# Four of six pieces of each expert's down matrix as fp16 halves in the gate-up ring, two as fp32 matmuls

## The chip, the cores and the metric

One core of one Trainium2 chip runs one inference step of a two-layer decoder. The metric is the time of one execution on the device in microseconds (us): 1238.76 us, the median of three runs (1237.88 to 1239.49). Lower is better.

## The reference

264 tokens (256 of a prompt and 8 samples) of width 1024 go through two layers. Each has a mixer, and then a feed-forward part: dense in the first layer, a mixture of experts in the second. Everything is fp32. What matters here is the mixture:

```python
def swiglu(x, w_gu, w_dn):
    g, u = jnp.split(x @ w_gu, 2, axis=-1)
    return (jax.nn.silu(g) * u) @ w_dn

def moe_swiglu(x, router, w_gu, w_dn):
    """Top-2-of-8 SwiGLU experts, softmax over the selected logits, per token."""
    ...
    for e in range(N_EXPERTS):
        out = out + comb[..., e:e + 1] * swiglu(x, w_gu[e], w_dn[e])
    return out
```

For each of the 8 experts `w_gu[e]` is 1024 x 3072 (12 MB) and `w_dn[e]` 1536 x 1024 (6 MB).

## The kernel before, in words

**Weights.** All weights come from memory as fp32 in pieces of 1 MB (128 partitions x 2048 numbers). Most are not multiplied as fp32. A piece is split: ScalarE writes the fp16 part of 256 times the weight to `wh` (`hi_gu`, L940), and VectorE the fp16 rest to `wl` (`lo_gu`, L1266). TensorE then does three fp16 matmuls for one product: high weight by high input, high weight by low input, low weight by high input (L844 to L846). `wh` and `wl` are a ring of four slots (`SLOTS`); a split waits until TensorE has used the piece four places before it (L939).

**One expert.** The matrix `w_gu[e]` is 12 pieces (`GU_U`), in three blocks of four; a piece has 96 matmuls with 128 weight columns against the expert's up to 96 tokens (`CAP`). From the sums in the four banks of `acc` ScalarE makes a tanh (`gates`, L1196) and VectorE the hidden values (`gate` L1762, `hidden_e` L1775, into `hid_e`, fp32, three parts q of four chunks). The matrix `w_dn[e]` is 6 pieces (`DN_U`). They are not split: `down` (L859) multiplies them as fp32, 96 columns of `hid_e` as weights and 512 columns of the piece moving, four matmuls a piece, straight from the slot where the transfer put it. There are six slots for gate-up pieces as loaded and five for down pieces.

**Order of work.** It is written out by hand and the same loop, for e from -1 to 7 and for turns g from 0 to 5, stands in each engine's program; an engine does its instructions in that order, and semaphores tie them together. In a turn TensorE does two gate-up pieces of expert e+1, and down piece g of expert e. In turns 0 and 1 it also scatters expert e-1's output back to the tokens (`scatter`, L805 and L806, two chunks before the down piece and two after), and VectorE adds these to the residual (`add_scattered`, L1751). In turn 2 TensorE gathers the tokens of expert e+2 (`gather`, L790 and L794, two banks before the down piece and two after), and ScalarE copies them out (`gathered`, L1180). Gathers, transposed selections (`by_token`, L724) and scatters take turns in two banks of `aux`: a fill waits until the one two before it has been read (`fill_bank`). In turn g ScalarE and VectorE split the gate-up pieces that are four ahead of the two that TensorE does. After turn 5 ScalarE scales the expert's output (L1229), in two halves, and VectorE makes its rest (`expert_out`, L1783), which the scatters of the next expert's turns and its first down piece wait for. The lines of ScalarE's program at this place, before the change:

```python
for g in range(DN_U):
    if e + 2 < NE and g == 3:
        gathered(e + 2, 2)
        gathered(e + 2, 3)
    for j in ((e + 1) * GU_U + 2 * g + SLOTS, (e + 1) * GU_U + 2 * g + SLOTS + 1):
        if j < GU_ALL:
            hi_gu(j)
    ...
    if e + 2 < NE and g == 2:
        gathered(e + 2, 0)
        gathered(e + 2, 1)
```

**Transfers.** SyncE's queue issues them in a fixed order: two gate-up pieces (L368), which wait for VectorE's split six pieces before, and a down piece (L382), which waits for TensorE's matmuls of the down piece five before. Fillers (`keep_warm`, L581) are fp16 matmuls of 512 columns whose result isn't used.

## Time and profile before

| | before |
|---|---|
| median of three runs | 1238.76 us (1237.88 to 1239.49) |
| the profiled execution | 1241.73 us |
| its span in the trace | 1240.1 us |
| TensorE busy | 1211.8 us (98%) |
| VectorE busy | 871.0 us (70%) |
| ScalarE busy | 629.4 us (51%) |
| clock granted to TensorE, of full | 0.979 |

The span is the part of the execution that the trace covers; all times in the rows count from its start. A row's duration of a matmul includes the time in the pipeline, so that matmuls that follow each other overlap, and the distance of two starts tells what one costs. The experts' loop runs from about 745 to 1190 us.

### The profile page before, as it was taken

Reading aid. Unit: us, or ns where it says so; the run is one execution under the profiler, and the core shown is the slowest. Engines: PE = TensorE matmul, PEld = TensorE weight load, DVE = VectorE, ACT = ScalarE, POOL = GpSimd, SP = SyncE. Lnnn points to the kernel's source line nnn. Section 1 sums busy time; section 2 is a strip of 40 time slices with the busy share of each in tenths; the row PEclk is TensorE's granted clock in tenths of the full one; section 3 lists DMA queues with packets and bytes.
Section 4 is the critical chain, followed back from the end, with each engine's and each line's share of the span. In section 5 each row is a group of like instructions: output and inputs, shape, how many; then the busy total and the mean of one; then the engine's idle time right before and its main releaser. Section 6 shows DMA issues by size and latency. Waiting matters only on the chain.

```text
span 1240.1 us, 27339 instructions
## 1 busy us (share of the span) xinstructions
PE 1211.8 (98%) x11977; PEld 957.4 (77%) x11977; DVE 871.0 (70%) x962; ACT 629.4 (51%) x613; POOL 24.9 (2%) x59
## 2 busy tenths in 40 slices
PE   7999999999999999999999989999999999999988
PEld 4888888878888887888888847876777777777556
DVE  5986886876666578977886785857557575747366
ACT  4555644455554455555744455645445454545233
POOL 4000000000000001000000000000000000000000
PEclk7999999999999999999999997999999999999999
DMA  9665665646555654465666647899898897988601
GB/s 263 204 218 189 203 202 181 200 136 204 194 185 197 204 170 153 137 204 181 202 199 203 238 157 282 328 370 384 314 374 330 318 400 307 376 325 328 235 1 36
DMA packets 171067, 289.31 MB, mean 233 GB/s; under 512 B 5195, under 2 KB 132187, under 8 KB 170954
## 3 DMA queue, kind: packets, MB, share of 16 engines
q1 hardware_dynamic: 169242, 283.71, 64.9%
q0 software_dynamic: 1728, 4.16, 1.2%
q8 instruction: 78, 1.28, 0.4%
q14 instruction: 19, 0.16, 0.0%
HBM read 286.53 MB, written 1.52 MB: 232 GB/s over the span
## 4 chain that ended last, share of the span: by engine, by line
PE 89%; DVE 7%; ACT 2%; issue 1%; DMA 0%; ACTq 0%; SPq 0%; DVEq 0%
PE acc L554 15%; PE acc L556 15%; PE acc L555 15%; PE aux L859 14%; PE acc L844 6%; PE acc L846 5%; PE acc L845 5%; PE aux L790 3%; PE acc L539 2%; PE acc L546 2%; PE acc L540 2%; DVE wl L1260 1%; DVE xb L1340 1%; PE aux L643 1%; DVE rstd L1321 1%; PE aux L594 1%
## 5 line engine op out<-in xcount | busy, mean ns | idle before, releaser
L554 PE MATMUL acc<-xn,wh 128*128 128x264 f16 x1424 | 393.0, 276 | 0.6 <-DVE wl L1260 0.6
L555 PE MATMUL acc<-xn,wh 128*128 128x264 f16 x1424 | 393.0, 276 | 0.0
L556 PE MATMUL acc<-xn,wl 128*128 128x264 f16 x1424 | 393.0, 276 | 0.0
L1260 DVE SCALAR_TENSOR_TENSOR wl<-raw,wh 128x2048 f16<-128x2048 f32 x124 | 283.5, 2289 | 104.9 <-ACT wh L931 104.4
L931 ACT ACTIVATE wh<-raw 128x2048 f16<-128x2048 f32 x124 | 235.6, 1903 | 0.1
L844 PE MATMUL acc<-ga,wh 128*128 128x96 f16 x1536 | 212.2, 212 | 0.2 <-issue 0.2
L845 PE MATMUL acc<-ga,wh 128*128 128x96 f16 x1536 | 212.0, 212 | 0.0
L846 PE MATMUL acc<-ga,wl 128*128 128x96 f16 x1536 | 212.0, 212 | 0.0
L1266 DVE SCALAR_TENSOR_TENSOR wl<-raw,wh 128x2048 f16<-128x2048 f32 x64 | 144.3, 2287 | 62.4 <-ACT wh L940 62.4
L940 ACT ACTIVATE wh<-raw 128x2048 f16<-128x2048 f32 x64 | 122.0, 1910 | 101.5 <-PE acc L846 97.8
L845 PEld LDWEIGHTS acc<-ga,wh 128*128 128x128 f16 x1536 | 155.6, 101 | 7.8 <-issue 7.6
L844 PEld LDWEIGHTS acc<-ga,wh 128*128 128x128 f16 x1536 | 155.5, 101 | 6.7 <-issue 6.4
L554 PEld LDWEIGHTS acc<-xn,wh 128*128 128x128 f16 x1424 | 139.3, 98 | 21.7 <-ACT wh L931 0.8
L555 PEld LDWEIGHTS acc<-xn,wh 128*128 128x128 f16 x1424 | 139.3, 98 | 21.1
L846 PEld LDWEIGHTS acc<-ga,wl 128*128 128x128 f16 x1536 | 155.6, 101 | 0.0
L556 PEld LDWEIGHTS acc<-xn,wl 128*128 128x128 f16 x1424 | 139.3, 98 | 20.9
L975 ACT ACTIVATE ot<-acc 128x528 f32<-128x528 f32 x47 | 28.6, 609 | 124.3 <-PE acc L556 97.3
L1266 DVE SCALAR_TENSOR_TENSOR wl<-sa,wh 128x2048 f16<-128x2048 f32 x16 | 36.7, 2291 | 44.4 <-ACT wh L940 44.4
L790 PE MATMUL aux<-ga,w 128*128 128x96 f16 (+1 forms) x384 | 46.1, 219 | 3.3 <-issue 3.2
L940 ACT ACTIVATE wh<-sa 128x2048 f16<-128x2048 f32 x16 | 30.6, 1910 | 36.8 <-PE acc L846 36.8
L790 PEld LDWEIGHTS aux<-ga,w 128*128 128x128 f16 (+1 forms) x384 | 27.2, 96 | 25.0 <-issue 6.9
L554 PE MATMUL acc<-w,wh 128*128 128x264 f16 x144 | 39.7, 276 | 0.0
(278 smaller groups left out, 1692.8 us busy)
## 6 DMA issues: line engine op xcount, KB each, us to landing
raw<-in_moe_w_gu SPq DMA_DIRECT2D x64, 1024.0 KB, 9.6
raw<-in_w_in SPq DMA_DIRECT2D x56, 1024.0 KB, 5.1
raw<-in_ffn_w_gu SPq DMA_DIRECT2D x24, 1024.0 KB, 5.2
sa<-in_moe_w_gu SPq DMA_DIRECT2D x16, 1024.0 KB, 8.5
xb<-in_moe_w_gu SPq DMA_DIRECT2D x16, 1024.0 KB, 10.4
raw<-in_ffn_w_dn SPq DMA_DIRECT2D x12, 1024.0 KB, 5.2
ya<-in_moe_w_dn SPq DMA_DIRECT2D x10, 1024.0 KB, 7.6
sg<-in_moe_w_dn SPq DMA_DIRECT2D x10, 1024.0 KB, 6.9
```

The costliest lines, as they stand in the source:

```text
L554: nc.tensor.matmul(bank, hi, x[:, 0, x0 + k, :], start=(k == 0), stop=False)
L555: nc.tensor.matmul(bank, hi, x[:, 1, x0 + k, :], start=False, stop=False)
L556: last = nc.tensor.matmul(bank, lo, x[:, 0, x0 + k, :], start=False, stop=(k == k_chunks - 1))
L790: last = nc.tensor.matmul(bank[:, at:at + CAP], nt[0:n, s, t, c * P:(c + 1) * P], sel[e % 2][0:n, t, :], start=(t == 0), stop=(t == 2))
L844: nc.tensor.matmul(bank, hi, x[:, 0, k, :], start=first, stop=False)
L845: nc.tensor.matmul(bank, hi, x[:, 1, k, :], start=False, stop=False)
L846: last = nc.tensor.matmul(bank, lo, x[:, 0, k, :], start=False, stop=end)
L859: last = nc.tensor.matmul(aux[0:CAP, 2 + half, :], hid_e[:, 2 * g + k, :], w[:, k, half * 512:(half + 1) * 512], start=(2 * g + k == 0), s ...
L931: nc.scalar.activation(wh[:, s, 0:size], raw_slot[s][:, 0:size], ACT.Copy, scale=WS).then_inc(hi_done, 1)
L940: nc.scalar.activation(wh[:, j % SLOTS, :], g_slot[j % G_SLOTS], ACT.Copy, scale=WS).then_inc(g_hi, 1)
L1260: op(V.scalar_tensor_tensor(out=wl[:, s, 0:size], in0=raw_slot[s][:, 0:size], scalar=WS, in1=wh[:, s, 0:size], op0=ALU.mult, op1=ALU.subtr ...
L1266: op(V.scalar_tensor_tensor(out=wl[:, j % SLOTS, :], in0=g_slot[j % G_SLOTS], scalar=WS, in1=wh[:, j % SLOTS, :], op0=ALU.mult, op1=ALU.su ...
```

## The change

The first four down pieces of each expert (`DN_HALVES`, g = 0 to 3) are split like gate-up pieces and take their places in the same ring of four slots, in the order in which TensorE uses the pieces: two gate-up pieces, then a down piece. ScalarE's and VectorE's splits of a turn are those four places ahead in this ring (`ring_ahead`), three in turns 0 to 3 and two in turns 4 and 5. The parts q = 0 and 1 of `hid_e` are split too (`hidden_hi` on ScalarE, `hidden_lo` on VectorE, into `hid_s`, which lies in `ot`). A split down piece is 12 fp16 matmuls (`down_halves`) instead of four fp32 ones; pieces g = 4 and 5 stay as they were. The slot of a split down piece is loaded again when VectorE has split it. The scale that takes back the 256 moves from `hid_e` to `csl`. What only renames `hid_e_ready` to `hid_made` is left out below.

```diff
+DN_HALVES = 4
+HC = 2 * DN_HALVES
+
+
+def in_halves(i):
+    return i % DN_U < DN_HALVES
+
+
+def half_ring():
+
+    order = [("g", j) for j in range(GU_U)]
+    for e in range(NE):
+        for g in range(DN_U):
+            if e + 1 < NE:
+                order += [("g", (e + 1) * GU_U + 2 * g + k) for k in range(2)]
+            if g < DN_HALVES:
+                order.append(("d", e * DN_U + g))
+    return order
+
+
+RING = half_ring()
+RING_AT = {key: n for n, key in enumerate(RING)}
+
+
+def ring_turn(e, g):
+
+    out = [("g", (e + 1) * GU_U + 2 * g + k) for k in range(2)] if e + 1 < NE else []
+    return out + ([("d", e * DN_U + g)] if e >= 0 and g < DN_HALVES else [])
+
+
+def ring_ahead(e, g):
+
+    turn = ring_turn(e, g)
+    if not turn:
+        return []
+    n = RING_AT[turn[0]] + SLOTS
+    return RING[n:n + len(turn)]
 
...
         mask_t, cum = var[0:NE, :], rtmp[0:NE, :]
+        hid_s = ot[:].rearrange("p a b t -> p (a b t)").bitcast(F16)[:, 0:2 * HC * CAP].rearrange("p (s c t) -> p s c t", s=2, c=HC)
         cmp_a, cmp_b = (x[:, 0:3 * NE * NE].rearrange("p (t m o) -> p t m o", t=3, m=NE) for x in (std, rstd))
...
         d_loaded = [sem(f"d_loaded{i}") for i in range(D_SLOTS)]
+        d_hi, d_lo, hid_hi, hid_lo = sem("d_hi"), sem("d_lo"), sem("hid_hi"), sem("hid_lo")
         g_hi, g_lo, gu_mm, dn_mm, y_half = sem("g_hi"), sem("g_lo"), sem("gu_mm"), sem("dn_mm"), sem("y_half")
 
+        def halves_to(i):
+
+            return i // DN_U * DN_HALVES + min(i % DN_U, DN_HALVES)
+
         block = ctx.enter_context(nc.Block())
...
                     sp.wait_ge(fill_full[0], 1)
+                elif in_halves(i - D_SLOTS):
+                    sp.wait_ge(d_lo, halves_to(i - D_SLOTS + 1))
                 else:
                 pe.wait_ge(g_lo, j + 1)
-                th = wh[:, j % SLOTS, :].rearrange("p (c m) -> p c m", c=2)
-                tl = wl[:, j % SLOTS, :].rearrange("p (c m) -> p c m", c=2)
+                slot = RING_AT["g", j] % SLOTS
+                th = wh[:, slot, :].rearrange("p (c m) -> p c m", c=2)
+                tl = wl[:, slot, :].rearrange("p (c m) -> p c m", c=2)
                 x = xg[e % 2]
...
 
+            def down_halves(i):
+
+                e, g = i // DN_U, i % DN_U
+                pe.wait_ge(hid_hi, HC // 4 * e + g // 2 + 1)
+                pe.wait_ge(hid_lo, HC // 4 * e + g // 2 + 1)
+                pe.wait_ge(d_hi, halves_to(i) + 1)
+                pe.wait_ge(d_lo, halves_to(i) + 1)
+                slot = RING_AT["d", i] % SLOTS
+                th = wh[:, slot, :].rearrange("p (c m) -> p c m", c=2)
+                tl = wl[:, slot, :].rearrange("p (c m) -> p c m", c=2)
+                for k in range(2):
+                    c = 2 * g + k
+                    for half in range(2):
+                        bank, s = aux[0:CAP, 2 + half, :], slice(half * 512, (half + 1) * 512)
+                        nc.tensor.matmul(bank, hid_s[:, 0, c, :], th[:, k, s], start=(c == 0), stop=False)
+                        nc.tensor.matmul(bank, hid_s[:, 0, c, :], tl[:, k, s], start=False, stop=False)
+                        last = nc.tensor.matmul(bank, hid_s[:, 1, c, :], th[:, k, s], start=False, stop=False)
+                last.then_inc(dn_mm, 1)
+
             def down(i):
...
                 e, g = i // DN_U, i % DN_U
-                pe.wait_ge(d_loaded[i % D_SLOTS], 16 * (i // D_SLOTS + 1))
-                pe.wait_ge(hid_e_ready, BLOCKS * e + g // 2 + 1)
                 if g == 0 and e:
                     pe.wait_ge(ys_ready, 2 * e)
+                if in_halves(i):
+                    down_halves(i)
+                    return
+                pe.wait_ge(d_loaded[i % D_SLOTS], 16 * (i // D_SLOTS + 1))
+                pe.wait_ge(hid_made, BLOCKS * e + g // 2 + 1)
                 w = d_slot[i % D_SLOTS].rearrange("p (c m) -> p c m", c=2)
...
             pe.wait_ge(fill_done[k % 2], k // 2 + 1)
-            pe.wait_ge(hid_e_ready, NE * BLOCKS)
             for c in range(C):
...
 
+            def ring_free(n):
+
+                kind, i = RING[n - SLOTS]
+                act.wait_ge(gu_mm if kind == "g" else dn_mm, i + 1)
+
             def hi(n, size=UNIT, it=None, step=0):
...
                 if n >= N_PLE[1]:
-                    act.wait_ge(gu_mm, GU_ALL - LEAD + (n - N_PLE[1]))
+                    ring_free(len(RING) + n - N_PLE[1])
                 elif n >= SLOTS:
...
                 act.wait_ge(g_loaded[j % G_SLOTS], 16 * (j // G_SLOTS + 1))
-                if j < SLOTS:
-                    act.wait_ge(unit_mm, N_MOE - LEAD + j)
+                n = RING_AT["g", j]
+                if n < SLOTS:
+                    act.wait_ge(unit_mm, N_MOE - LEAD + n)
                 else:
-                    act.wait_ge(gu_mm, j - LEAD)
-                nc.scalar.activation(wh[:, j % SLOTS, :], g_slot[j % G_SLOTS], ACT.Copy, scale=WS).then_inc(g_hi, 1)
+                    ring_free(n)
+                nc.scalar.activation(wh[:, n % SLOTS, :], g_slot[j % G_SLOTS], ACT.Copy, scale=WS).then_inc(g_hi, 1)
+
+            def hi_dn(i):
+
+                act.wait_ge(d_loaded[i % D_SLOTS], 16 * (i // D_SLOTS + 1))
+                n = RING_AT["d", i]
+                ring_free(n)
+                nc.scalar.activation(wh[:, n % SLOTS, :], d_slot[i % D_SLOTS], ACT.Copy, scale=WS).then_inc(d_hi, 1)
+
+            def hidden_hi(e, q):
+
+                act.wait_ge(hid_made, BLOCKS * e + q + 1)
+                nc.scalar.activation(hid_s[:, 0, 4 * q:4 * q + 4, :], hid_e[:, 4 * q:4 * q + 4, :], ACT.Copy,
+                                     scale=1.0 / WS).then_inc(hid_hi, 1)
 
                         gathered(e + 2, 3)
-                    for j in ((e + 1) * GU_U + 2 * g + SLOTS, (e + 1) * GU_U + 2 * g + SLOTS + 1):
-                        if j < GU_ALL:
-                            hi_gu(j)
+                    for kind, i in ring_ahead(e, g):
+                        if kind == "g":
+                            hi_gu(i)
+                        else:
+                            hi_dn(i)
                     if e + 1 < NE and g == 1:
...
                         by_token(e + 2)
+                    if e + 1 < NE and g in (4, 5):
+                        hidden_hi(e + 1, g - 4)
                     if e == NE - 1 and g in (2, 3, 4):
...
                 vec_e.wait_ge(g_hi, j + 1)
-                op(V.scalar_tensor_tensor(out=wl[:, j % SLOTS, :], in0=g_slot[j % G_SLOTS], scalar=WS,
-                                          in1=wh[:, j % SLOTS, :], op0=ALU.mult, op1=ALU.subtract), g_lo)
+                slot = RING_AT["g", j] % SLOTS
+                op(V.scalar_tensor_tensor(out=wl[:, slot, :], in0=g_slot[j % G_SLOTS], scalar=WS, in1=wh[:, slot, :],
+                                          op0=ALU.mult, op1=ALU.subtract), g_lo)
+
+            def lo_dn(i):
+
+                vec_e.wait_ge(d_hi, halves_to(i) + 1)
+                slot = RING_AT["d", i] % SLOTS
+                op(V.scalar_tensor_tensor(out=wl[:, slot, :], in0=d_slot[i % D_SLOTS], scalar=WS, in1=wh[:, slot, :],
+                                          op0=ALU.mult, op1=ALU.subtract), d_lo)
+
+            def hidden_lo(e, q):
+
+                vec_e.wait_ge(hid_hi, HC // 4 * e + q + 1)
+                op(V.scalar_tensor_tensor(out=hid_s[:, 1, 4 * q:4 * q + 4, :], in0=hid_e[:, 4 * q:4 * q + 4, :],
+                                          scalar=1.0 / WS, in1=hid_s[:, 0, 4 * q:4 * q + 4, :], op0=ALU.mult,
+                                          op1=ALU.subtract), hid_lo)
 
...
                 vec_e.wait_ge(fill_done[k % 2], k // 2 + 1)
-                op(V.tensor_tensor(csl[0:CAP, e:e + 1], csr[0:CAP, e, 0:1], csr[0:CAP, e, 1:2], ALU.add), csl_ready)
+                op(V.tensor_scalar(csl[0:CAP, e:e + 1], csr[0:CAP, e, 0:1], csr[0:CAP, e, 1:2], UNSCALE, ALU.add, ALU.mult),
+                   csl_ready)
 
...
                 op(V.scalar_tensor_tensor(out=hid_e[:, 4 * q:4 * q + 4, :].rearrange("p c t -> p (c t)"), in0=w,
-                                          scalar=0.5 * UNSCALE * UNSCALE, in1=acc[:, block % 2 * 2 + half, 0:GW],
-                                          op0=ALU.mult, op1=ALU.mult), hid_e_ready)
+                                          scalar=0.5 * UNSCALE, in1=acc[:, block % 2 * 2 + half, 0:GW],
+                                          op0=ALU.mult, op1=ALU.mult), hid_made)
 
...
                                           in1=ye[0:CAP, 0, s], op0=ALU.mult, op1=ALU.subtract), ys_ready)
+
+            def split(kind, i):
+                if kind == "g":
+                    lo_gu(i)
+                else:
+                    lo_dn(i)
 
...
                 for g in range(DN_U):
-                    first = (e + 1) * GU_U + 2 * g + SLOTS
+                    ahead = ring_ahead(e, g)
                     if g == 0 and 2 <= e + 2 < NE:
...
                         slot_weights(e + 2)
-                    if first < GU_ALL:
-                        lo_gu(first)
+                    if ahead:
+                        split(*ahead[0])
                     if e >= 1 and g < 2:
...
                         add_scattered(e - 1, 4 * g + 1)
-                    if first + 1 < GU_ALL:
-                        lo_gu(first + 1)
+                    for key in ahead[1:]:
+                        split(*key)
                     if e + 1 < NE:
...
                             hidden_e(block, 0)
+                        if g in (4, 5):
+                            hidden_lo(e + 1, g - 4)
                     if e >= 1 and g < 2:
```

## Rows read from the trace of the kernel before

**Rows 1.** The page: busy time of TensorE, its share and instructions.

```profile
PE 1211.8 (98%) x11977; PEld 957.4 (77%) x11977; DVE 871.0 (70%) x962; ACT 629.4 (51%) x613; POOL 24.9 (2%) x59
```

**Rows 2.** Busy time by stretch, from one expert's first gate-up piece to the next.

```profile
core 0: us, PE busy (x) PEld busy (x) DVE busy (x) ACT busy (x) POOL busy (x), PEclk, DMA share, GB/s
895.98:950.71 54.73, 54.73 (x696) 39.11 (x694) 34.62 (x33) 27.49 (x23) 0.00 (x0) 0.97 0.89 349
```

**Rows 3.** Waits in 895.98 to 950.71: engine, line, releaser; us, times, longest.

```profile
ACT wh L940 <- PE acc L846: 19.9, 7, 4.5
DVE wl L1266 <- ACT wh L940: 14.8, 6, 4.8
```

**Rows 4.** Timeline of TensorE: start, duration, line, operation, shapes, count.

```profile
884.95 3.64 PE L859 MATMUL aux<-ya,w 128*96 128x512 f32 x8
...
888.43 0.21 PE L844 MATMUL acc<-ga,wh 128*128 128x96 f16 x1
...
892.51 3.64 PE L859 MATMUL aux<-sg,w 128*96 128x512 f32 x8
...
916.90 2.74 PE L790 MATMUL aux<-ga,w 128*128 128x96 f16 x24
...
923.08 2.74 PE L790 MATMUL aux<-ga,w 128*128 128x96 f16 x24
...
926.06 0.22 PE L844 MATMUL acc<-ga,wh 128*128 128x96 f16 x1
...
931.75 0.41 PE L724 MATMUL aux<-identh,ga 128*96 128x128 f16 x3
```

**Rows 5.** Timeline of TensorE, one run of fillers.

```profile
735.03 1.91 PE L581 MATMUL acc<-identh 128*128 128x512 f16 x8
```

**Rows 6.** Instructions of line L724: durations ns min/median/max.

```profile
L724 PEld LDWEIGHTS aux<-identh,ga x24: 114/123/195, 753.0 to 1096.1; 128*96 128x96 f16 x16, 8*96 8x96 f16 x8
```

**Rows 7.** Groups of instructions by line in 895.98 to 950.71: busy us, mean ns.

```profile
L845 PEld LDWEIGHTS acc<-ga,wh 128*128 128x128 f16 x192 | 19.4, 101 | 1.0 <-issue 1.0
```

**Rows 8.** Timeline of VectorE.

```profile
913.74 1.01 DVE L1762 SCALAR_TENSOR_TENSOR w<-w,acc 128x384 f32<-128x384 f32 x2
914.67 0.76 DVE L1751 SCALAR_TENSOR_TENSOR h<-aux,h 128x264 f32<-128x264 f32 x2
917.07 4.49 DVE L1266 SCALAR_TENSOR_TENSOR wl<-raw,wh 128x2048 f16<-128x2048 f32 x2 [1.64 <-ACT wh L940]
...
1167.67 0.77 DVE L1751 SCALAR_TENSOR_TENSOR h<-aux,h 128x264 f32<-128x264 f32 x2 [2.91 <-PE aux L806]
```

**Rows 9.** Timeline of ScalarE.

```profile
918.98 0.47 ACT L1180 ACTIVATE ga<-aux 128x384 f16<-128x384 f32 x1
...
1162.15 0.68 ACT L1229 ACTIVATE gb<-aux,csl 96x512 f16<-96x512 f32 x1 [0.97 <-PE aux L859]
1162.74 5.50 ACT L931 ACTIVATE wh<-raw 128x2048 f16<-128x2048 f32 x3
```

**Rows 10.** Timeline of TensorE near the end of the experts.

```profile
1167.36 0.27 PE L806 MATMUL aux<-gb 96*128 96x264 f16 x1
1167.47 0.28 PE L805 MATMUL aux<-gb 96*128 96x264 f16 x1
...
1168.16 0.29 PE L805 MATMUL aux<-gb 96*128 96x264 f16 x1 [0.30 <-DVE h L1751]
```

**Rows 11.** Busy time by stretch, columns as in rows 2 (PEclk: granted clock).

```profile
740.00:760.00 20.00, 16.38 (x168) 12.15 (x169) 4.88 (x16) 9.26 (x15) 0.00 (x0) 0.66 0.80 310
...
926.00:932.00 6.00, 6.00 (x100) 5.91 (x100) 0.46 (x2) 2.46 (x3) 0.00 (x0) 0.72 1.02 416
```

**Rows 12.** Waits of the queue that issues transfers, 700 to 1190.

```profile
SPq L382 <- PE aux L859: 305.4, 43, 11.1
```

**Rows 13.** Busy time of one short stretch, columns as in rows 2.

```profile
908.00:912.00 4.00, 4.00 (x28) 2.09 (x25) 3.35 (x4) 3.28 (x4) 0.00 (x0) 1.00 1.02 410
```

More of the change, by code:

```diff
@@ L89 @@
 FILL = aux_fills()
+DN_HALVES = 4
[13 more added lines that the diff above has]
+RING_AT = {key: n for n, key in enumerate(RING)}
+assert len(RING) % SLOTS == 0
+def ring_turn(e, g):
[7 more added lines that the diff above has]
+    return RING[n:n + len(turn)]
 def program(nc, a, o):
@@ L213, in program @@
         d_loaded = [sem(f"d_loaded{i}") for i in range(D_SLOTS)]
+        d_hi, d_lo, hid_hi, hid_lo = sem("d_hi"), sem("d_lo"), sem("hid_hi"), sem("hid_lo")
         g_hi, g_lo, gu_mm, dn_mm, y_half = sem("g_hi"), sem("g_lo"), sem("gu_mm"), sem("dn_mm"), sem("y_half")
-        tanh_done, gate_free, hid_e_ready = sem("tanh_done"), sem("gate_free"), sem("hid_e_ready")
+        tanh_done, gate_free, hid_made = sem("tanh_done"), sem("gate_free"), sem("hid_made")
         fill_full = [sem(f"fill_full{i}") for i in range(2)]
@@ L826, in gate_up @@
                     else:
-                        pe.wait_ge(hid_e_ready, BLOCKS * before + 2 * b - 1)
+                        pe.wait_ge(hid_made, BLOCKS * before + 2 * b - 1)
                 if u == 0:
@@ L1193, in gates @@
                 if block and block % BLOCKS == 0:
-                    act.wait_ge(hid_e_ready, block)
+                    act.wait_ge(hid_made, block)
                 at = (block % BLOCKS * 2 + half) * GW
```

## The prediction

> **What bounds the kernel now.** I read the page's busy shares first: TensorE is busy for 98% of the span [rows 1]. Then the stretches of single experts: from one expert's first gate-up piece to the next it is 54.73 us, TensorE has no idle time in it, VectorE works 34.6 and ScalarE 27.5 us, the granted clock is 0.97 and the 16 DMA engines are 0.89 busy at 349 GB/s [rows 2]. So experts are bound by TensorE. The waits say how close the others are: ScalarE waits 19.9 us for TensorE to free a slot of the ring, VectorE 14.8 us for ScalarE, per expert [rows 3]. The other engines are early, but only by what the ring lets them be, and that is what the change touches.
>
> **What the change takes from TensorE.** A down piece of four fp32 matmuls shows as eight instructions, 884.95 to 888.43, 3.48 us; a pair of gate-up pieces 888.43 to 892.51, 4.08 us, 2.04 each [rows 4]. The new piece is 12 fp16 matmuls of 512 columns. Such matmuls stand in the trace as fillers: eight in 1.91 us with a last one of 0.38 are 7 steps in 1.53, 0.218 us each [rows 5], so 2.61 us a piece and 0.87 less than now. 4 pieces x 8 experts x 0.87 = 27.8 us off TensorE.
> Its weights have 96 columns. A fp16 load of that width takes 0.12 us [rows 6]; hidden under 0.218 of matmul it costs nothing, wholly exposed 12 x 0.12 = 1.44 a piece and 46 us in all. I take nothing: the gate-up matmuls, at 4.08/96 = 0.043 each, run over loads of 0.10 [rows 4, 7]. Below nothing it can't go, as the twelve steps are the fillers' own.
> The Trainium skill (TensorE: Matmul & The Clock Gate, Back-to-back issue gap) gives about 131 ns for a sustained 512-column matmul. By it a piece would be 1.57 us. The fillers here contradict it; it stands as a rival below.
>
> **What it adds elsewhere.** 32 splits on ScalarE at 1.80 us from start to start (three in 5.50 with a last of 1.91) and on VectorE at 2.20 (two in 4.49, the last 2.29) [rows 8, 9]; 16 small ones of hid_e on each, which I price like a gate of 384 columns, 0.46 (two in 1.01) [rows 8]. VectorE then works 34.6 + 4 x 2.2 + 2 x 0.46 = 44.3 us per expert, ScalarE 27.5 + 4 x 1.8 + 0.8 = 35.5, against 54.73 - 4 x 0.87 = 51.25 of TensorE. On the average it fits. But the ring has still four slots and now three pieces a turn (g = 0 to 3) where there were two, so a piece is split 1.3 turns ahead, not 2. Both engines take work in written order, so other things queue behind a split that waits. Latencies: from the end of a matmul's slot to its dependant 0.2 us (L805 at 1167.47 follows the L806 of 1167.36; VectorE starts at 1167.67), ScalarE to VectorE 0.04, VectorE to TensorE 0.05 (the add started 1167.67 is 0.43 long, L805 at 1168.16) [rows 8, 10].
>
> **Stall A, certain by the order.** In turn g = 2 ring_ahead gives pieces g7 and g8 of expert e+1 and d3 of e, in the order g7, d3, g8. g8 takes the slot of d2, which is this turn's own down piece. ScalarE has gathered(e+2, 0) behind that split, and TensorE's gather 2, which follows d2 directly, waits for it because it writes the same bank. After d2 ends: 0.2 + 1.81 (split) + 0.48 (gathered, 0.47 long) [rows 9] + 0.05 = 2.55 us of idle TensorE. Before, both splits of that turn wait for gate-up pieces only, and gathered starts at 918.98, 4.1 us ahead of gather 2 at 923.08 [rows 4, 9]. Experts e = 0 to 5 have it: 6 x 2.55 = 15.3 us.
>
> **Stall B.** In turn g = 1 the last split, g6, takes the slot of d1. Behind it on VectorE stand two gates and add_scattered 6; gather 0 of the next turn wants the bank of that add. After d1: 0.2 + 1.91 + 0.04, split 2.20, two gates 0.92, add 0.42 [rows 8], 0.05: 5.74. TensorE gets there after four scatter matmuls (0.11 each [rows 10]) and a gate-up pair: 0.45 + 4.08 = 4.53. Stall 1.2, for e = 1 to 5: 6.0 us.
>
> **Stall C.** Scatter matmuls of turns 0 and 1 need VectorE's adds for their banks, and the adds stand behind splits. From the end of the expert before, turn 0 runs: VectorE ends a last split at 1.0 and does hidden by 1.5; ScalarE halves it by 2.1, scales two halves of the output (0.6 each, 0.68 long [rows 9]) by 3.3 and splits g3 by 5.2; VectorE splits it by 7.4 and adds by 7.8. TensorE would want that bank at 4.08 + 0.45 + 2.61 = 7.1: stall 0.7. Then VectorE: add 1 8.2, two splits 12.6, add 2 13.0; TensorE 7.8 + 0.6 + 4.08 = 12.5: 0.5. With the second adds of each pair (0.1 each) 1.3 per expert, for e = 1 to 6: 7.8 us. Bounds per expert 0, if the chain starts 1 us sooner, and 2.6, if it starts 1.3 later.
>
> **Ends.** In the first expert VectorE starts behind, as gate-up alone asks 2.20 of it per 2.04 of TensorE; with d0 (2.2) and two hidden splits (0.5 each) on top g15 is late by about 2.8. At e = 6 the scale of the expert's output (ScalarE L1229 [rows 9]) is queued behind hidden_hi(7, 1), which waits for VectorE's hidden, itself behind three splits: about 3 us more than now. Together 5.8, bounds 0 and 9.
>
> **Clock.** At 926.06 a gate-up pair takes 5.69 instead of 4.08; the clock in 926 to 932 is 0.72, part of it at the lower of the two levels, 1.2 GHz, right after gather (24 matmuls from 916.90), down and gather (from 923.08) [rows 4, 11]. There are five such places (e = 1 to 5), 1.6 us each, 8 us. The stretch from the first gather is lengthened by 2.55 of idle and has Stall B ahead of it. In 740 to 760, with TensorE busy 16.4 of 20 us, it was 0.66 [rows 11]. So I expect seven or eight drops for five: +4 us. Bounds: -8 (none, because the fp16 piece between the gathers keeps the clock) and +16 (two per expert).
>
> **Transfers.** SP waits 305 us at L382 for down pieces that TensorE has read [rows 12]; four of six slots are now free at the split, before the matmuls. An expert's 18 pieces of 1.05 MB take 18.9 / 0.40 = 47 us at the 400 GB/s of a stretch in which the DMA engines are full (410 at a share of 1.02) [rows 13], under 51. I count nothing. If they sustained only the mean of 349 GB/s [rows 2]: 54 us, and no gain could come whatever the engines do.
> UNSCALE moved into csl, one tensor_scalar for a tensor_tensor, one wait less at the end of the experts: nothing, under VectorE's idle time there.
>
> **Sum.** -27.8 + 15.3 + 6.0 + 7.8 + 5.8 = +7.1; with the clock +11. The profiled execution took 1241.73 us with a span of 1240.1; it becomes 1252.8, which stands as that one did 3.0 over the median. Forecast 1238.8 + 11.1 = 1250 us. Range of this case alone 1243 to 1262.
>
> **Rivals.**
> 1. *The other engines keep up* (ends on the other side). VectorE's 44.3 of 51 us per expert fits, B, C and the ends vanish, only A stays: -27.8 + 15.3 = -12.5, with the clock as it is 1226 us. For it: 14.8 us of waiting per expert in which VectorE has nothing to do [rows 3]. Against it: those waits are for slots, and slots are scarcer now. It decides once B, C and the ends together stay under 8.5 us, where I have 19.6. 9%.
> 2. *The clock stays up.* With A to C as above and no drop at all: 1238.8 + 7.1 - 8 = 1238: no change. For it: dense fp16 instead of fp32 between the gathers. Against: more idle. 7%.
> 3. *Weight loads are exposed.* 0.12 a matmul makes the piece 4.05: 32 x 0.57 = 18 dearer than the old one where a gain of 28 stood, while A stays and some of B and C is covered: 1238.8 + 18 + 15 + 10 = 1282 us. For it: 24 gather matmuls of 96 columns take 2.74 us, 0.11 each, where gate-up's take 0.043 [rows 4]. Against: these change between 128 and 8 rows, the new ones don't. 5%.
> 4. *The page's 131 ns.* TensorE gives back 32 x 1.91 = 61 us, but VectorE and the slots then bind: of the further 33 us about half is waited away, 1233 us. 2%, since the fillers show 0.218.
> 5. *Transfers bind*: at 349 GB/s 54 us plus the drops, 1250 to 1258; not to be told from the forecast by time, only by ScalarE waiting on DMA. 7%.
> The forecast has 70%.
>
> **Chances.** A measurement of this kernel can tell about 0.2%, 2.5 us. Slower: the forecast (nearly all), 3 and 5: 81%. Same: 2 and the lowest edge of the forecast: 8%. Faster: 1 and 4: 11%. Range 1238 to 1264: it leaves out rival 1, 3 and 4 and the tails.
>
> **What would show it.** In the expert stretches: the period from gate-up to gate-up about 56 to 57 us instead of 54.73; down pieces of 2.6 us in g = 0 to 3; TensorE idle 2.5 us after d2, released by ScalarE's ga (L1180's successor); 1.2 us before gather 0 and under a microsecond before scatters, released by VectorE's adds; VectorE over 80% busy. Wrong would be: no idle time before gather 2, a period under 53 us, down pieces of 3.5 us or more, or ScalarE's splits waiting for DMA.

## The result and the profile after

The changed kernel takes 1270.48 us, median of four executions (1266.84 to 1275.58), against 1239.12 before (four executions as well): ratio 1.0254 [1.0225, 1.0282]. In a later set of runs the same kernel took 1272.97 us (1267.25 to 1275.64), ratio 1.0264 [1.0224, 1.0303]. Forecast were 1250 us and 1238 to 1264: slower, as said, but by 31 us instead of 11, and outside the range. The profile below is of the fastest of the four executions; the second profile, of the later set, is of the slowest there (1275.64).

The page of the changed kernel, to be held against [rows 1]: span, busy time, and the chain that ended last.

```profile
span 1265.2 us, 27755 instructions
PE 1201.7 (95%) x12105; PEld 966.9 (76%) x12105; DVE 950.4 (75%) x1010; ACT 693.1 (55%) x661; POOL 24.9 (2%) x59
...
PE 73%; DVE 19%; ACT 5%; issue 1%; DMA 1%; ACTq 0%; SPq 0%; DVEq 0%
```

The span grew by 25.1 us (from 1240.1). TensorE's busy time fell by 10.1 (from 1211.8), and its idle time, span less busy, rose from 28.3 to 63.5, by 35.2. Forecast were 34.9 us of stalls in sum, and busy time at -23.8 (saving and clock together). So the miss is in busy time, which fell by far less than the matmuls give back; the sum of the stalls came out, though not each of its terms.

One expert, gate-up to gate-up (busy time by stretch, columns as in [rows 2]), with the row of two short stretches in it:

```profile
1020.91:1078.93 58.02, 53.60 (x712) 40.02 (x711) 44.51 (x39) 35.30 (x29) 0.00 (x0) 0.94 0.85 324
1044.00:1048.00 4.00, 4.00 (x21) 2.05 (x20) 3.54 (x2) 0.00 (x0) 0.00 (x0) 0.61 0.92 329
1050.00:1052.00 2.00, 0.00 (x0) 0.00 (x0) 0.18 (x1) 2.00 (x2) 0.00 (x0) 1.00 1.02 412
1055.00:1059.00 4.00, 4.00 (x56) 3.97 (x57) 0.21 (x1) 0.55 (x2) 0.00 (x0) 0.57 0.83 266
```

The expert of 54.73 us [rows 2] now takes 58.02, with 4.42 us of idle TensorE. VectorE's 44.5 and ScalarE's 35.3 us of work are as reckoned (44.3, 35.5). The clock falls in two places, after gather 0 (third column from the right: 0.61) and after gather 2 (0.57), partly to the lower level, 1.2 GHz; before it fell in one [rows 11].

The waits of the same stretch (engine, line, releaser; us, times, longest). Before, TensorE had no idle time in an expert [rows 2].

```profile
ACT wh L1016 <- PE aux L914: 9.3, 4, 6.1
...
PE aux L838 <- ACT ga L1269: 2.4, 1, 2.4
...
PE aux L838 <- DVE h L1860: 1.1, 1, 1.1
PE aux L853 <- DVE h L1860: 0.9, 2, 0.6
```

L838 is the gather, L1016 the split of a gate-up piece on ScalarE, L914 the last matmul of a down piece in halves. L853 is the scatter. The first row is the cause of Stall A, the second Stall A itself, the third Stall B, the fourth Stall C. In the timelines (start, duration, line) Stall A is read from TensorE to ScalarE and back; first TensorE, from gather 0, which Stall B made late, to gather 2:

```profile
1042.86 3.00 PE L838 MATMUL aux<-ga,w 128*128 128x96 f16 x24 [1.12 <-DVE h L1860]
...
1047.94 0.54 PE L914 MATMUL aux<-wh,ot 128*96 128x512 f16 x1
1048.33 0.38 PE L912 MATMUL aux<-wh,ot 128*96 128x512 f16 x1
1048.54 0.38 PE L913 MATMUL aux<-wl,ot 128*96 128x512 f16 x1
...
1049.40 0.38 PE L914 MATMUL aux<-wh,ot 128*96 128x512 f16 x1
1052.22 1.41 PE L838 MATMUL aux<-ga,w 128*128 128x96 f16 x12 [2.44 <-ACT ga L1269]
```

and ScalarE:

```profile
1049.88 1.91 ACT L1016 ACTIVATE wh<-raw 128x2048 f16<-128x2048 f32 x1 [6.14 <-PE aux L914]
1051.70 0.85 ACT L1269 ACTIVATE ga<-aux 128x384 f16<-128x384 f32 x2
```

The last matmul of d2 ends, ScalarE splits g8 (1.8 us), only then copies the gathers out (L1269), and gather 2 starts 2.44 us late. At full clock the matmuls of the piece follow each other by 0.215 us, as the fillers of [rows 5] did. The Trainium skill (TensorE: Matmul & The Clock Gate, Back-to-back issue gap) has about 131 ns for a sustained 512-column matmul; this trace does not agree, and rival 4 falls.

At e = 6 ScalarE's timeline shows the chain of the tail:

```profile
1182.00 1.91 ACT L1023 ACTIVATE wh<-ya 128x2048 f16<-128x2048 f32 x1 [3.36 <-DMA ya<-in_moe_w_dn]
1186.73 0.52 ACT L1028 ACTIVATE ot<-w 128x384 f16<-128x384 f32 x1 [2.82 <-DVE w L1884]
1187.16 1.24 ACT L1322 ACTIVATE gb<-aux,csl 96x512 f16<-96x512 f32 x2
```

The split of d45 (L1023; d45 is down piece g = 3 of expert 7, pieces counted from 0) waits for its transfer, whose slot ya came free only when the fp32 piece d40 (L930) had been multiplied. Behind it stand hidden_hi (L1028) and the output scale (L1322). The transfer queue's wait (1140 to 1190), and TensorE's for the scale (1175 to 1215):

```profile
SPq L430 <- PE aux L930: 12.0, 2, 7.2
```

```profile
PE aux L853 <- DVE gb L1892: 6.6, 1, 6.6
```

### The profile page after: what moved, and what is told of

It is laid out like the page before. It is cut to its first block, busy times and chain, and to the rows that moved or that the text cites. A ratio compares the mean times of both kernels' runs of the same rounds, so it can differ in the third digit from the quotient of the medians.

```text
span 1265.2 us, 27755 instructions
## 1 busy us (share of the span) xinstructions
PE 1201.7 (95%) x12105; PEld 966.9 (76%) x12105; DVE 950.4 (75%) x1010; ACT 693.1 (55%) x661; POOL 24.9 (2%) x59
## 4 chain that ended last, share of the span: by engine, by line
PE 73%; DVE 19%; ACT 5%; issue 1%; DMA 1%; ACTq 0%; SPq 0%; DVEq 0%
PE acc L602 15%; PE acc L604 15%; PE acc L603 15%; DVE wl L1360 6%; PE aux L838 4%; DVE wl L1367 3%; PE acc L893 3%; PE acc L895 3%; PE acc L894 3%; PE aux L930 2%; PE aux L912 2%; ACT wh L1016 2%; PE acc L587 2%; PE acc L594 2%; PE acc L588 2%; PE aux L913 2%
## 5 line engine op out<-in xcount | busy, mean ns | idle before, releaser
L893 PE MATMUL acc<-ga,wh 128*128 128x96 f16 x1536 | 213.0, 212 | 2.8 <-DVE wl L1360 2.5
L893 PEld LDWEIGHTS acc<-ga,wh 128*128 128x128 f16 x1536 | 155.8, 101 | 7.7 <-issue 6.4
L1016 ACT ACTIVATE wh<-raw 128x2048 f16<-128x2048 f32 x64 | 121.3, 1907 | 65.6 <-PE aux L914 45.1
L838 PE MATMUL aux<-ga,w 128*128 128x96 f16 (+1 forms) x384 | 48.8, 228 | 23.6 <-ACT ga L1269 14.6
L838 PEld LDWEIGHTS aux<-ga,w 128*128 128x128 f16 (+1 forms) x384 | 27.1, 98 | 47.1 <-ACT ga L1269 17.7
L912 PE MATMUL aux<-wh,ot 128*96 128x512 f16 x128 | 52.1, 407 | 0.2 <-DVE wl L1367 0.2
L913 PE MATMUL aux<-wl,ot 128*96 128x512 f16 x128 | 51.6, 403 | 0.0
L914 PE MATMUL aux<-wh,ot 128*96 128x512 f16 x128 | 51.1, 399 | 0.0
```

Source lines behind the costliest of these rows:

```text
L838: last = nc.tensor.matmul(bank[:, at:at + CAP], nt[0:n, s, t, c * P:(c + 1) * P], sel[e % 2][0:n, t, :], start=(t == 0), stop=(t == 2))
L893: nc.tensor.matmul(bank, hi, x[:, 0, k, :], start=first, stop=False)
L912: nc.tensor.matmul(bank, hid_s[:, 0, c, :], th[:, k, s], start=(c == 0), stop=False)
L1016: nc.scalar.activation(wh[:, n % SLOTS, :], g_slot[j % G_SLOTS], ACT.Copy, scale=WS).then_inc(g_hi, 1)
```

## The experiments

**Gathered ahead of the third split** (ScalarE, turn 2):

```diff
-                    for kind, i in ring_ahead(e, g):
+                    for n, (kind, i) in enumerate(ring_ahead(e, g)):
+                        if e + 2 < NE and g == 2 and n == 2:
+                            gathered(e + 2, 0)
+                            gathered(e + 2, 1)
```

> The changed kernel, but in turn 2 ScalarE does gathered(e+2, 0) and (e+2, 1) before the split of the third piece instead of behind it. Theory 1 (the idle time of TensorE after d2, stall A, is a queueing matter of ScalarE, and it also brings on one of the two drops of the clock per expert): A's 2.55 us for six experts and one drop of 1.5 us for about six are gone, 15 + 9: about 1246 us, period of an expert 54.0 instead of 58.0, clock 0.97 in it. Rival 2 (A is only such a matter, but the drops come from the sparse gathers themselves): 15 us less, 1255, two drops stay. Rival 3 (the split of the third piece, which now starts later, makes TensorE wait elsewhere): less than 8 us gained.

Measured: 1242.29 us, ratio to before 1.0026 [1.0006, 1.0045], 28 us under the changed kernel. Waits of TensorE in one expert (1061.11 to 1115.19), of which Stall A is missing and Stall B is left, and the expert as a stretch:

```profile
PE aux L838 <- DVE h L1863: 1.1, 1, 1.1
PE aux L853 <- DVE h L1863: 0.8, 2, 0.6
```

```profile
1061.11:1115.19 54.08, 52.10 (x711) 38.69 (x710) 44.41 (x39) 35.41 (x29) 0.00 (x0) 0.97 0.92 353
```

Idle time per expert fell from 4.42 to 1.98 us, six times 2.44 = 14.6 us. The other 13.5 us between the two medians are left for the clock: 0.97 in this expert and two others, 0.91 and 0.94 in the remaining two, where the changed kernel has 0.94 four times and 0.91 once.

**Adds ahead of the third split** (VectorE, turns 0 and 1):

```diff
-                    for key in ahead[1:]:
+                    for n, key in enumerate(ahead[1:]):
+                        if n == 1 and e >= 1 and g < 2:
+                            add_scattered(e - 1, 4 * g + 2)
+                            add_scattered(e - 1, 4 * g + 3)
                         split(*key)
```

> The changed kernel, but in turns 0 and 1 VectorE does the second pair of add_scattered before the split of the third piece (and before the gates) instead of behind both. Theory 1: stall B (1.3 us before gather 0) and the second part of stall C (0.5) go, 0.3 comes at the last scatters: 7 to 8 us less, about 1262 us, A and the clock's drops stay as they are. Rival 2 (VectorE is simply too busy, and order does not matter): the third split is later, g6 makes TensorE wait as long as gather 0 did, no gain.

Measured: 1258.65 us, 1.0152 [1.0119, 1.0185]. An expert as a stretch:

```profile
1016.48:1072.44 55.96, 52.83 (x712) 39.53 (x711) 44.43 (x39) 35.42 (x29) 0.00 (x0) 0.94 0.88 333
```

The waits of TensorE in it, and the next expert:

```profile
PE aux L838 <- ACT ga L1269: 2.4, 1, 2.4
PE aux L853 <- DVE h L1860: 0.6, 1, 0.6
```

```profile
1072.44:1130.62 58.18, 54.53 (x712) 40.05 (x711) 44.42 (x39) 35.42 (x29) 0.00 (x0) 0.91 0.86 327
```

Idle 3.13 us: Stall B and part of C are gone, A stands, and the clock stays at 0.94 or lower.

**Both orders:**

> Both reorderings of the two runs before in one kernel. Theory 1: the stalls add up (22 us less with A and B), with the drop of the clock that A brings on 30 less: 1238 to 1241 us, period 52.5 (50.9 without a drop of the clock). Rival 2 (drops stay two): 1247 us. Rival 3 (VectorE at 44.5 of 51 us is the next limit): period over 54 us with VectorE 85% busy and TensorE waiting for its splits.

Measured: 1230.40 us, 0.9927 [0.9898, 0.9957]: faster than before by 0.7%, and 8 us under what was expected. One of four experts of 50.9 us, and the fifth:

```profile
991.96:1042.89 50.93, 50.24 (x711) 37.95 (x710) 44.32 (x39) 35.42 (x29) 0.00 (x0) 1.00 0.98 372
1042.89:1098.25 55.36, 53.60 (x711) 40.20 (x710) 44.33 (x39) 35.53 (x29) 0.00 (x0) 0.94 0.90 343
```

The same 711 matmuls as in the changed kernel take 50.24 us of busy time where they took 53.60. That is the clock's share there: 3.36 us per expert. In these four experts the clock is above the 0.97 of the kernel before too. The fifth has the stalls of the others and one stop more, 1.07 us in the middle of gather 0, which the profile lays to no engine; it has the busy time of an expert of the changed kernel again.

**The matmuls alone**, in the kernel before (pieces 0 to 3 of each expert are 12 fp16 matmuls on the normalised tokens; their true product is left out, and nothing is split for them):

```diff
+                if g < 4:
+                    for k in range(2):
+                        c = 2 * g + k
+                        for half in range(2):
+                            for t in range(3):
+                                last = nc.tensor.matmul(aux[0:CAP, 2 + half, :], nt[:, 1, 0, c * CAP:(c + 1) * CAP],
+                                                        nt[:, 1, 1, half * 512:(half + 1) * 512], ...)
```

> The kernel before, in which the four fp32 matmuls of down pieces 0 to 3 are 12 fp16 matmuls with the same 96 weight columns and 512 moving columns, but on parts of the tokens that are already there in fp16: nothing is split for them, the ring is as before, and the experts' output is left out of the computation for these pieces. Theory 1 (the matmuls give back what was reckoned, all of the loss lies in queues and clock): 32 x 0.88 = 28 us less, 1211 us, and if the denser work between the gathers keeps the clock up, up to 8 less: 1203. Rival 2 (clock drops come with fp16 pieces between gathers, not with idle time): 1211 + 5 to 9 us with two drops per expert. Rival 3 (the transfers bind as soon as an expert takes less than 51 us): period over 51.5 and ScalarE waiting for DMA.

Measured: 1208.22 us, 0.9751 [0.9725, 0.9777].

```profile
935.33:985.01 49.68, 49.68 (x711) 38.27 (x710) 34.57 (x33) 27.38 (x23) 0.00 (x0) 1.00 0.98 383
```

An expert of before at full clock is 53.12 (55.52 in the first row of the kernel before with fillers, below, less its 2.40 of fillers), so four pieces give 3.44 us, 27.5 for eight experts where 27.8 were reckoned. The DMA engines bring an expert's pieces in 49.7 us: rival 5 falls. They are 0.98 busy in that, so they come next. The time fell by 30.3 us, 2.8 more than the saving, and only two of five experts still have a low stretch, one each (51.28 and 51.27 us at 0.97). So fp16 pieces between the gathers bring none by themselves.

**Stall A filled** (the wait stays, its idle time is given to fillers):

```diff
                     if e + 2 < NE and g == 2:
+                        if e >= 0:
+                            pe.wait_ge(gate_free, e + 2)
+                            keep_warm(11, acc[:, (BLOCKS * (e + 1)) % 2 * 2, :])
                         gather(e + 2, 2)
```

> The changed kernel with 11 fillers of 512 columns (0.218 us each, 2.40 us together) issued on TensorE right before gather 2, in the 2.55 us in which it otherwise waits for ScalarE's gathered (Stall A). Every wait stays as it is, and the fillers fit into the idle time, so the sum of stalls is unchanged. They only take TensorE's idleness away there. Theory 1 (the lower clock that follows stall A is brought by the idle time of the stall): the half-clock stretch that begins about 2 to 4 us after gather 2 goes, some 1.5 us for each of 7 experts, and the period of experts 3 to 6 falls from 58.0 to about 56.4 us: about 1260 us. Theory 2 (the sparse gathers, 24 matmuls of 96 columns in 2.7 us each, bring it, whatever stands in between): unchanged, 1270 us, period 58.0. If the fillers end later than gathered comes, each expert costs up to 0.2 us more.

Measured: 1264.33 us, 1.0208 [1.0181, 1.0235]. The three short stretches that answer to those of the changed kernel, 2.5 to 3 us earlier, and the expert:

```profile
1041.50:1045.50 4.00, 4.00 (x19) 2.03 (x18) 3.23 (x2) 0.00 (x0) 0.00 (x0) 0.61 0.95 333
1047.00:1049.00 2.00, 2.00 (x11) 0.88 (x9) 0.00 (x0) 1.84 (x2) 0.00 (x0) 1.00 1.02 408
1052.00:1056.00 4.00, 4.00 (x51) 3.88 (x50) 0.21 (x1) 0.55 (x2) 0.00 (x0) 0.57 0.82 262
1018.10:1076.26 58.16, 56.13 (x722) 41.21 (x721) 44.51 (x39) 35.31 (x29) 0.00 (x0) 0.94 0.86 326
```

The second is full now, and the clock falls in the first and third as it did; busy time is that of the changed kernel's expert, 53.6, and the fillers. Against Theory 1, as far as Stall A alone goes. The median is 6 to 9 us less all the same, and the four executions (1262.92 to 1265.07) lie below all eight of the changed kernel (1266.84 to 1275.64): that suggests that only the surplus of the slower ones went, which have longer low stretches (below, the changed kernel again).

**Adds first, and Stall A filled** (both diffs above):

> VectorE's order as in the kernel with adds first (1258.65 us: no Stall B, Stall A left), and the 11 fillers in the idle time of Stall A. Then TensorE has hardly any idle time left in an expert, while it waits as long as with adds first. Theory 1 (idle time of either stall brings the low clock; where only one was filled, the other kept it up): the low stretches go as in the kernel with both orders, period 54 us instead of 55.9 to 58.1, 1243 to 1247 us. Theory 2 (it is the length of the stretch of sparse and waiting work around the gathers, or their place in time, and fillers can't undo it): 1256 to 1260 us as with adds first.

Measured: 1244.07 us, 1.0055 [1.0038, 1.0072], 14.6 us under the kernel with adds first, which waits just as long.

```profile
1009.53:1064.68 55.15, 54.42 (x723) 40.58 (x721) 44.42 (x39) 35.41 (x29) 0.00 (x0) 0.97 0.90 342
1064.68:1118.23 53.55, 52.81 (x722) 38.97 (x721) 44.42 (x39) 35.41 (x29) 0.00 (x0) 1.00 0.93 354
```

Its five experts are of these two kinds, 53.6 or 55.2 us; those of adds first took 55.9 to 58.2. Less 2.4 of fillers TensorE is busy 52.0 and 50.4 us in the two rows, where adds first has 52.83 and 54.53. So idle time does bring the low clock: where both stalls are out, filled or undone, it is mostly gone; where one is left, it stays in part (gathered first, B left: 0.97 in three of five experts) or in whole (adds first, A left: 0.91 to 0.94; Stall A filled, B left: 0.94).

**The kernel before with the same fillers:**

> The kernel before with 11 fillers ahead of gather 2, so that the two groups of gathers lie as far apart as in the changed kernel, with no idle time and no split of down pieces. TensorE gets 11 x 0.218 = 2.4 us more per expert, six times or seven: +14.4 to +16.8 us, 1253 to 1256 us, if the low clock stays one stretch per expert. Theory 2 (the distance between the gathers makes two stretches of one): +1.5 x 6 = 9 more, 1262 to 1265. If more dense work takes the stretch away: 8 less, 1245 to 1248.

Measured: 1250.75 us, 1.0107 [1.0077, 1.0136]. Two experts:

```profile
897.98:953.50 55.52, 55.52 (x707) 38.57 (x706) 34.57 (x33) 27.50 (x23) 0.00 (x0) 1.00 0.89 343
953.50:1010.62 57.12, 57.12 (x706) 40.19 (x705) 34.56 (x33) 27.39 (x23) 0.00 (x0) 0.97 0.87 332
```

With and without a low stretch they differ by 1.60 us, the price used in the forecast. Dense work between the gathers took the low stretch from three of the five experts that had one, and added none: the distance of the gathers is not what doubled it.

**Two pieces in halves instead of four** (`DN_HALVES = 2`, `HC = 8`), and **three** (`DN_HALVES = 3`, `HC = 8`):

> The changed kernel with two down pieces of an expert in halves (g = 0, 1) instead of four, the hidden parts as before. Turn 2 then splits the two gate-up pieces alone, so gathered(e+2, 0) is no longer behind a split that waits for this turn's own down piece: Stall A gone. Stall B and C remain as turns 0 and 1 are unchanged. Saving 16 x 0.87 = 13.9 us instead of 27.8. Theory 1 (stalls by the order of the ring, and clock drops that follow them): per expert -1.74 + B 1.2 + C 1.3 with one clock drop of 1.6 as before or up to two, period 55 to 56.5, in all 1238 to 1252 us, likeliest 1243. Theory 2 (load on VectorE and ScalarE as such sets the time): each piece costs about (1270 - 1238.5)/4 = 8 us, so 1254 us.

> The changed kernel with three down pieces of an expert in halves (g = 0, 1, 2). The third split of turn 2 (g8, into the slot of d2) is back and with it Stall A. Saving 24 x 0.87 = 20.9 us. Theory 1: A comes as a step between two and three pieces, so this one lies 15.3 - 7.0 = 8 us above the kernel with two pieces before clock drops, and with the second drop per expert that follows A (1.5 us x 7) 15 to 20 us above it: 1256 to 1268 us; and slower or as slow as with four (1270 minus nothing: four adds one more saving of 7.0 but also VectorE's work in turn 3). Theory 2 (load as such): on a line between two and four, 1262 us with two at 1254; the step from two to three is then no larger than that from three to four.

Measured: two 1248.16 us, 1.0068 [1.0044, 1.0093]; three 1271.26, 1.0272 [1.0243, 1.0302]. An expert of each; the one with two pieces is the shortest of its five (54.5 to 57.3 us, idle 1.97 to 2.20, clock 0.94 to 1.00):

```profile
956.87:1011.32 54.45, 52.25 (x703) 37.63 (x702) 40.30 (x37) 31.93 (x27) 0.00 (x0) 1.00 0.91 349
```

```profile
1027.94:1087.71 59.77, 55.35 (x708) 39.87 (x707) 42.31 (x38) 33.62 (x28) 0.00 (x0) 0.91 0.86 322
```

The third piece costs 23 us, the fourth nothing: not load, but the order that puts Stall A in. Idle time goes from about 2.0 to 4.42 us per expert and the clock from 0.94 to 1.00 down to 0.89 to 0.91. I had 1256 to 1268 for three; it was 3 over. The fourth piece should still save 7 us; part of that is lost in the tail, where the kernel with three pieces, which does not split d45, waits for the output scale (1180 to 1215) 1.3 us instead of 6.6:

```profile
PE aux L853 <- DVE gb L1892: 1.3, 1, 1.3
```

**The tail alone**: in the changed kernel's last turn of e = 6 the split of d45 stands behind the output scales and expert_out.

```diff
+                    late = e == NE - 2 and g == DN_U - 1
-                    for kind, i in ring_ahead(e, g):
+                    for kind, i in ring_ahead(e, g)[:1 if late else None]:
...
+                if e == NE - 2:
+                    hi_dn(ring_ahead(e, DN_U - 1)[1][1])
```

> The changed kernel with one move: in the last turn of e = 6 the split of d45, on ScalarE and on VectorE, stands behind that expert's output scales and expert_out. Nothing else is touched. Theory 1 (the 6.6 us that TensorE waits at the first scatter of e = 6 come from the scale queued behind that split, which waits for its transfer and its slot): the wait falls to 1 to 2 us, 4 to 5 us less in all, span up to the first scatter after the last fp32 down piece 10.2 -> 5.5 us. Rival (hidden_hi(7, 1), which waits for VectorE's hidden behind other splits, holds it all the same): about 1 us less. The clock's own changes between executions (1266.84 to 1275.58 for the same kernel) may cover it, so it is read in the trace.

Measured: 1269.04 us, 1.0240 [1.0209, 1.0270]. The time alone says nothing; the waits of TensorE in 1180 to 1215 do:

```profile
PE aux L853 <- DVE h L1863: 1.5, 2, 1.3
PE aux L853 <- DVE gb L1895: 1.3, 1, 1.3
```

6.6 us became 1.3, but the scatters' waits for adds grew from 0.3 to 1.5, so that 4.1 us are gained, as Theory 1 had it (4 to 5). In the time this does not show, as the clock of this profile was 0.957 and that of the changed kernel's first 0.970.

**The changed kernel again:**

> The changed kernel unchanged, to see how far its low-clock stretches differ between executions: its four executions were 1266.84, 1273.97, 1275.58 and 1266.99 us at granted clocks of 0.970, 0.961, 0.956 and 0.969, while Stall A, B and C are fixed by the order. Theory 1 (the stalls fix 1257 us, and the rest is the clock): a profile with another time shows the same waits to a few tenths of a us and differs in the number and length of the low stretches alone. Rival (waits for transfers or engines change between executions): the waits differ.

Measured: 1272.97 us. Its profiled execution has a span of 1274.0. TensorE's waits in the expert from 964.53 to 1025.14, and that expert:

```profile
PE aux L838 <- ACT ga L1269: 2.4, 1, 2.4
PE aux L838 <- DVE h L1860: 1.1, 1, 1.1
PE aux L853 <- DVE h L1860: 0.9, 2, 0.6
```

```profile
964.53:1025.14 60.61, 56.19 (x711) 41.05 (x710) 44.51 (x39) 35.30 (x29) 0.00 (x0) 0.89 0.82 315
988.00:995.00 7.00, 6.89 (x24) 3.03 (x22) 3.17 (x2) 0.01 (x1) 0.00 (x0) 0.51 0.95 364
998.00:1005.00 7.00, 7.00 (x72) 5.67 (x72) 1.43 (x2) 1.04 (x3) 0.00 (x0) 0.53 0.47 153
```

The same waits, the same idle 4.42 us, and 2.6 us more of busy time for the same matmuls, at a clock of 0.89 for 0.94. There are still two low stretches, after gather 0 (986.49) and after gather 2 (997.33), but they are longer: 0.51 and 0.53 over 7 us each. That is Theory 1 inside the experts. In the tail the rival has a part: the transfer of d45 came later, and TensorE's wait for the scale (1140 to 1220) was 8.4 us for 6.6.

```profile
PE aux L853 <- DVE gb L1892: 8.4, 1, 8.4
```

**What the runs point to**: both orders, the tail's move, and hidden part 1 halved in turn 0 of its own expert, behind the output scales.

```diff
-                    if e + 1 < NE and g in (4, 5):
-                        hidden_hi(e + 1, g - 4)
+                    if e + 1 < NE and g == 4:
+                        hidden_hi(e + 1, 0)
+                    if e >= 0 and g == 0:
+                        hidden_hi(e, 1)
```

> Both orders turned round (gathered of e+2 ahead of the third split of turn 2, VectorE's second pair of adds ahead of the third split), and two further moves: hidden part 1 is halved in turn 0 of its own expert behind the output scales instead of at the end of the expert before, and in the last turn of e = 6 the split of d45 is queued behind that expert's output scale and expert_out. Theory 1 (what remained in the kernel with both orders is the chain that delays the adds and, at e = 6, the scatter): period 50.4 instead of 50.9 us, tail 4 to 5 us shorter: from 1230 to 1218 to 1224 us. Rival (what remains there is TensorE's own work and a few clock drops): 1228 to 1231 us, no change to the kernel with both orders.

Measured: 1221.37 us (1218.26 to 1227.11), 0.9877 [0.9850, 0.9903]: faster than the kernel before by 1.2%, and than the one with both orders. All of TensorE's waits in the experts, 838 to 1140:

```profile
PE aux L853 <- DVE h L1868: 3.0, 6, 0.5
PE aux L838 <- issue: 1.5, 2, 1.0
```

## Why the prediction was wrong

| us against before | reckoned | first profile | second profile |
|---|---|---|---|
| saving | -27.8 | -27.5 | -27.5 |
| clock | +4 | +17.4 | +27.6 |
| TensorE busy | -23.8 | -10.1 | +0.1 |
| Stall A | +15.3 | +14.6 | +14.6 |
| Stall B | +6.0 | +5.6 | +5.6 |
| Stall C | +7.8 | +5.4 | +5.4 |
| Ends | +5.8 | +9.6 | +8.2 |
| TensorE idle | +34.9 | +35.2 | +33.8 |
| span | +11.1 | +25.1 | +33.9 |

Busy and idle are from the pages (second profile: busy 1211.9 of 1274.0). The saving is that of the matmuls alone, the clock is the rest of busy. Stalls A to C are the waits of the whole profile (740 to 1220; the second has the same three), and the Ends are the rest of idle:

```profile
PE aux L838 <- ACT ga L1269: 14.6, 6, 2.4
PE aux L838 <- DVE h L1860: 5.6, 5, 1.1
PE aux L853 <- DVE h L1860: 5.4, 13, 0.6
PE acc L893 <- DVE wl L1360: 2.5, 1, 2.5
```

- **The step that failed is Clock**: "So I expect seven or eight drops for five: +4 us." It was two stretches in each expert, in the second profile longer ones, and 17 to 28 us. Of the 14.0 us by which the first span grew more than forecast, 13.4 are the clock. The bounds were wrong as well: +16 took a drop as 1.6 us, the price of one in a kernel with no stalls [rows 2, 11]. In three of the five experts of the second profile the clock costs 56.19 - 50.24 = 5.95 us, more than two such. The forecast priced the clock by counting events; what it had seen in [rows 11] (0.66 where TensorE was busy 16.4 of 20 us, 0.72 after the gathers) pointed at idle time and sparse work together, and the change put 3.6 us of idle time (A and B) into every expert right at the gathers. The kernels with both orders and with adds first and A filled show that this idle time is what does it. And the range ended at 1264, while the forecast's own terms with its own bound came to 1238.8 + 7.1 + 16 = 1262: the range left no room for a bound that was a guess.
- **Ends** was short by 3.8 in the first profile. The first scatter of e = 6 waited 6.6 us where "about 3" stood: the transfer of d45 was not in the chain, as its slot was taken to be free early, while this one is freed by a fp32 piece, late. g15 was late by 2.5 us (L893 above), 2.8 reckoned.
- **Stall A**: 2.44 us of idle time, 2.55 reckoned, from the rows alone, and undone by one move of order, as the rival order shows. **Stall B**: 1.1 for 1.2. **Stall C**: 0.9 for 1.3. That idle time in sum came out at 35.2 for 34.9 is partly luck, as C was 2.4 too high and Ends 3.8 too low.
- **The saving** and the price of the splits (no exposed weight loads, 0.215 us a matmul) held: rivals 3 and 4 fall. Rival 1 falls with the idle time. Rival 2 (the clock stays up) was the opposite of what happened. Of the signs to look for, two did not come: the period was 58.0 us for "56 to 57", and up to 60.6, and VectorE was busy 44.5 of 58.0 us in an expert, 77%, for "over 80%". The down pieces took 2.6 us only at the full clock; the d2 shown above, partly at the low one, took 4.

What the forecast took for two terms is one: with both orders the stalls fell by 4.42 - 0.69 = 3.73 us per expert, 22 for six, and the time by 40. The 18 us more are the clock's.

**Open**: why the low clock stayed in the changed kernel when Stall A alone was filled, while with B undone the same fillers took most of it away; why two executions with the same stalls in the experts differ by 10 us of clock; and what stopped TensorE for 1.07 us in the fifth expert with both orders. Two such stops, of 1.0 and 0.5 us, stand in the last kernel too, in experts whose clock stayed at 1.00, so that a stop of this size does not always bring the low clock. The fillers were not tried in Stall B.

## What to carry to other kernels

Before a buffer ring is shared by more pieces, write down for each turn whose slot each split takes; where it is this turn's own, everything behind it on that engine waits, and what another engine needs from it goes ahead of it. Here that one move of order was worth 28 us, as much as the matmuls' saving (27.5). A stall beside sparse TensorE work can cost more than its idle time: reckon the clock as a share of the stall, and put its bound wider than the stall itself (here 3.4 to 6.0 us of clock for 4.4 of idle time in an expert).

## What was not expected of the hardware

- Short stalls at the gathers brought as much clock as idle time: 711 matmuls of an expert took 50.24 us of busy time with 0.69 us idle, 53.60 and 56.19 with 4.42 us idle.
- The granted clock of a kernel is not the same from one execution to the next: 0.956 to 0.970 and 1266.84 to 1275.64 us in the changed kernel, with equal Stalls A to C in the two executions profiled. It is no matter of stalls alone: the kernel before ranged from 1234.53 to 1242.11 us at 0.979 to 0.988, and the one with Stall A filled only over 2.2 us.
- More work can cost less than its time: 14.4 us of fillers in the kernel before made it 12.7 us longer.
